# Activation stores two tiles ahead, and another order of loads, eviction and casts at the change of halves

## The reference, cut to what matters

```python
h = rmsnorm(x, g_pre) * (1 + scale[:, None]) + shift[:, None]
z = h @ w_in
a_conv, g_conv, q, k, v, g_attn, qi, ki, wi, gm = split_in(z)
y_c, conv_new = conv_branch(a_conv, conv_prev, conv_w, conv_b, ln_g, ln_b)
y_c = (y_c * jax.nn.silu(g_conv)) @ w_conv_out
o = sparse_attention(q, k, v, qi, ki, wi, past, rel_bias)
y_a = (o * jax.nn.silu(g_attn)) @ w_attn_out
gm_c, gm_a = jnp.split(jax.nn.sigmoid(gm), 2, axis=-1)
y = rmsnorm((gm_c * y_c + gm_a * y_a) @ w_out, g_post)
return x + gate[:, None] * y, conv_new, k, v, ki
```

## Time and profile before

| | us |
|---|---|
| median of 3 runs | 3480.4 (3471.67 to 3483.89) |
| the profiled execution | 3479.13 |
| its span in the trace | 3477.5 |
| PE busy | 3268.8 (94%) |
| DVE busy | 2691.2 (77%) |
| ACT busy | 1466.0 (42%) |
| POOL busy | 1037.6 (30%) |

### The profile page before, as it was taken

How to read it: one execution, slowest core, us unless ns; L and a number is a source line. 1 busy time by engine, 2 the same in 40 slices (tenths; PEclk the granted TensorE clock), 3 DMA queues, 4 the chain that set the end, 5 groups by cost and what they waited for, 6 DMA issues and landing times. The chain is left out here.

```text
span 3477.5 us, 50401 instructions
## 1 busy us (share of the span) xinstructions
PE 3268.8 (94%) x19461; PEld 3008.9 (87%) x19461; DVE 2691.2 (77%) x4071; ACT 1466.0 (42%) x1961; POOL 1037.6 (30%) x885
## 2 busy tenths in 40 slices
PE   6999999999999999999998999898999989999998
PEld 3889888999999899999996777777777779989987
DVE  2432788998989899999995888898898875886444
ACT  2312567988930100010004666676676650323121
POOL 2222111453335300000003443543533324664200
PEclk9999999999999999999999999999999999999999
DMA  7265534545555643344444322323221235667443
GB/s 262 76 181 161 150 118 130 165 148 191 174 187 183 250 151 145 141 170 156 166 147 109 91 56 65 80 56 86 57 61 52 58 112 179 202 210 267 136 145 112
DMA packets 381524, 485.53 MB, mean 140 GB/s; under 512 B 49296, under 2 KB 304464, under 8 KB 379685
## 3 DMA queue, kind: packets, MB, share of 16 engines
q1 hardware_dynamic: 324133, 288.19, 27.7%
q10 hardware_dynamic: 46960, 152.90, 12.5%
q0 software_dynamic: 10256, 42.23, 3.0%
HBM read 301.98 MB, written 184.13 MB: 140 GB/s over the span
## 5 line engine op out<-in xcount | busy, mean ns | idle before, releaser
L1126 PE MATMUL psum<-ha,gt 128*128 128x352 f32 x8136 | 1350.9, 324 | 5.1 <-DVE ha L1402 3.6
L1126 PEld LDWEIGHTS psum<-ha,gt 128*128 128x128 f32 x8136 | 1321.1, 188 | 8.7 <-DVE ha L1402 3.8
L1438 DVE SCALAR_TENSOR_TENSOR cv<-cv,vecs,cv 128x1056 f32<-128x1056 f32 (+1 forms) x480 | 607.7, 1346 | 0.0
L1912 ACT CAST at<-psum 128x1024 fp32r<-128x1024 f32 (+2 forms) x308 | 288.9, 938 | 318.8 <-PE psum L1823 318.5
L1986 DVE TENSOR_TENSOR at<-psum,at 128x1024 fp32r<-128x1024 f32 (+2 forms) x308 | 345.9, 1127 | 80.2 <-ACT at L1912 78.3
L1823 PE MATMUL psum<-ident,at 128*128 128x128 f32 (+1 forms) x2320 | 346.5, 276 | 39.8 <-ACT at L1893 30.3
L1842 PE MATMUL psum<-at,at 128*128 128x512 f32 (+1 forms) x1160 | 343.2, 399 | 27.3 <-ACT at L1920 26.8
L1823 PEld LDWEIGHTS psum<-ident,at 128*128 128x128 f32 (+1 forms) x2320 | 275.8, 143 | 102.3 <-ACT at L1893 37.7
L703 PE MATMUL psum<-br,br 128*128 128x352 f32 x2016 | 340.6, 330 | 14.9 <-DVE br L2359 10.7
L703 PEld LDWEIGHTS psum<-br,br 128*128 128x128 f32 x2016 | 334.0, 192 | 18.6 <-issue 12.0
L777 DVE TENSOR_SCALAR_CACHE_REDUCE gl<-gt,gl 128x1792 bf16<-128x1792 f32 (+8 forms) x263 | 337.7, 1350 | 1.2
(11 more groups left out here) (253 smaller groups left out, 4143.3 us busy)
## 6 DMA issues: line engine op xcount, KB each, us to landing
scratch_ws<-gt SPq DMA_DIRECT2D x112, 512.0 KB, 4.0
gt<-scratch_ws ACTq DMA_DIRECT2D x110, 512.0 KB, 5.0
gt<-in_w_in_dram SPq DMA_DIRECT2D x60, 512.0 KB, 5.8
scratch_gm<-gt ACTq DMA_DIRECT2D x32, 528.0 KB, 3.0
br<-scratch_gm ACTq DMA_DIRECT2D x32, 528.0 KB, 3.8
scratch_m<-br POOLq DMA_DIRECT2D x32, 528.0 KB, 5.1
at<-scratch_q SPq DMA_DIRECT2D x128, 128.0 KB, 2.9
scratch_u<-gl POOLq DMA_DIRECT2D x16, 528.0 KB, 4.2
```

The costliest lines, as they stand in the source:

```text
L1126: return nc.tensor.matmul(of[:, j, 0:W // 3], part[:, c, :], a[:, c, j * (W // 3):(j + 1) * (W // 3)], start=(c == 0 and k == 0), stop=(c ...
L1438: ins = nc.vector.scalar_tensor_tensor(to[:, 0:width], mine[:, k_:k_ + width], tap, to[:, 0:width], ALU.mult, ALU.add)
L1912: nc.scalar.copy(phi[j % 3][:, 0:len(mine), 0:n], turned[j % 2][:, 0:len(mine), 0:n]).then_inc(s_phi, 1)
```

## The change

In the front stage SP's step `t` issues `hidden(t + 2)` instead of `hidden(t + 1)`; since tiles below 8 are not stored, the first store moves from step 7 to step 6.

In the gate stage ACT issues `fetch(BLOCKS + 1)` ahead of the eviction of block `BLOCKS - 2` instead of behind it and behind `fetch(BLOCKS)`. This fetch now waits for the store of the block that it reads, no longer for the last store of split weights. In `next_acts` all casts stand behind the eighth load, so that the eviction of the last block stands ahead of every cast.

```diff
--- before.py
+++ after.py
@@ -321,8 +321,8 @@
                 if t >= 1:
                     key_columns(t - 1)
                 key_rows(t)
-                if t + 1 < NTL:
-                    hidden(t + 1)
+                if t + 2 < NTL:
+                    hidden(t + 2)
                 if 0 <= t - FREE < len(LOADS):
                     query_weights(t - FREE)
             key_columns(NT)
@@ -1266,10 +1266,10 @@
                         act.wait_ge(pr.s_split, QI - E + BLOCKS)
                     else:
                         act.wait_ge(pr.s_mm, QI - E + (j - 2 if j == BLOCKS + 2 else j - 1))
-                    if j <= BLOCKS + 2:
+                    if j == BLOCKS or j == BLOCKS + 2:
                         act.wait_ge(s_wst[0 if j == BLOCKS else 1], 16 * BLOCKS)
                     if j == BLOCKS + 1:
-                        act.wait_ge(s_wst[0], 32)
+                        act.wait_ge(s_wst[1], 32)
                     done = s_wfirst[j - BLOCKS - 1] if BLOCKS < j <= BLOCKS + 2 else s_wld[j % 2]
                     for k, part in enumerate(later(j)):
                         act.dma_start(part[:].rearrange("p c f -> p (c f)").bitcast(F32), scr["ws"][j - BLOCKS, k]).then_inc(done, 16)
@@ -1283,10 +1283,7 @@
                         act.wait_ge(pr.s_mm, QI - E + BLOCKS)
                         evict(BLOCKS // 2 - 1, 1)
                     act.dma_start(alo[:, c, :].bitcast(F32), scr["h"][:, c, W:2 * W]).then_inc(s_act[c], 16)
-                    if c >= 3 and c < KC - 1:
-                        next_high(c - 3)
-
-                for c in range(KC - 4, KC):
+                for c in range(KC):
                     next_high(c)
 
             def next_high(c):
@@ -1337,10 +1334,11 @@
                 if j == BLOCKS - 1:
                     next_acts()
                 else:
+                    if j == BLOCKS - 2:
+                        fetch(BLOCKS + 1)
                     evict(j // 2, j % 2)
                 if j == BLOCKS - 2:
                     fetch(BLOCKS)
-                    fetch(BLOCKS + 1)
                 elif j == BLOCKS - 1:
                     fetch(BLOCKS + 2)
                 elif j > BLOCKS:
```

## The result

| | median us | ratio to the kernel before, 95% interval |
|---|---|---|
| first comparison, 4 runs each | 3453.2, before 3479.5 | 0.9930 (0.9912 to 0.9948) |
| again, 7 runs against 12, on another occasion | 3459.7, before 3478.6 | 0.9952 (0.9936 to 0.9969) |

The change is a gain of 0.5 to 0.7%: 26 us by the first comparison (interval 18 to 31), 19 by the second (11 to 22). The forecast was 3460, a gain of 19.0. The profiled execution of the first comparison took 3456.8 us, span 3455.1; that of before 3479.1. The two traces therefore differ by 22.4 us of span.

The account below looks back on a forecast made before the run. In the front, late-issued stores of h held DVE's modulate and so PE; at the change of halves PE waited for ACT's eviction behind casts. Savings 15.3 + 3.7 = 19.0 us from 3479.1 gave 3460 us; range 3450 to 3471.

Parts of the forecast that it names:

- The waits for `h` go: Front stage: issuing the store of h a tile sooner removes all 22.4 us of DVE's modulate waits.
- What is late next in the front: Tiles 9 to 16: PE's steps of 52.8 us plus two delays make 55.3 instead of 70.6; 15.3 us saved.
- root chain: Front: scale factors of tiles 12 to 15, made on DVE behind modulate(11), delay PE by 1.8 us.
- second weight block: Front: ACT's cast of the second early weight block waits for its load, tile 14's cast queues behind; 0.7 us.
- Edit 2: Change of halves: spare weights fetched first; nothing on PE's path by itself, later activation rows some 1.3 us sooner.
- Edit 3: Change of halves: eviction before casts; one PE gap of 4.4 us replaces 3.56 and 5.13, pair ends 5.1 us sooner.
- The dump: After the pair: weights ACT fetches beside POOL's mask dump come late, cutting the 5.1 us gain to 3.7.
- The other reading: At the dump: if DMA queues' turns were equal in bytes, weights come in time and the gain is 5.1 us.
- (a): Rival: only the front counts, dump or landings take the whole gain at the change of halves; 3464; chance 0.12.
- (c): Rival: key outputs' round on SP, about 9.5 us a tile, bounds the front, not the stores; 3471; chance 0.08.
- (b): Rival: short gaps remain in the front and the clock falls in two; front 10.4, in all 14; 3465; chance 0.12.
- (d): Rival: ACT's seventh load stalls at issue, delaying eviction, clock low for the pair; 10.5 us slower, 3490; chance 0.03.

Follow-up runs that it names:

- e5: Kernel before with one swap in SP's front-stage step: the store of h (still tile t + 1) ahead of the key rows; one run, 3462.8 us.
- e8: Changed kernel plus two front edits: root chain ahead of modulate on DVE, second early weight block cast one step later on ACT; 3452.1 us, ratio 0.9917.
- e3: Kernel before with only the casts moved behind the eviction, spare weights' fetch left where it was; 3471.5 us, ratio 0.9990.
- e4: Kernel before with only the spare weights' fetch ahead of the eviction and its loosened wait, casts as before; 3473.7 us, ratio 0.9988.
- e14: Changed kernel with the mask dump in four stores, one behind each of blocks 3 to 6 of half two; one run, 3457.7 us.
- e15: e3 with the mask dump in four stores, one behind each of blocks 3 to 6 of half two; one run, 3461.9 us.
- e2: Kernel before with both gate-stage edits (spare weights first, eviction ahead of casts), without the front's edit; 3472.4 us, ratio 0.9988.
- e12: The changed kernel repeated unaltered against the kernel before on the same chip; 3459.7 us, ratio 0.9952.
- e9: e3 with the mask dump cut into eight stores of 4.6 KB a row instead of one of 37 KB a row; one run, 3477.2 us.

## Why the prediction was right, step by step

- **The waits for `h` go.** Right: 22.4 us to none, and e5 shows that the loop of modulation, copies, issues and landing was the bound and the key outputs were not.
- **What is late next in the front.** 15.3 was forecast as 70.6 - 55.3; the stretch is 55.7 to 56.1 in the four kernels with this edit and the old delays, 14.6 to 14.9 less than before. The term for the root chain, 1.8, measured 1.82 in all four. That for the second weight block, 0.7, measured 0.95 to 1.32; it was the term that was too small, and it follows the landing: from issue to cast that load took 5.15 us before and 5.57 to 5.95 in the four. e8 takes both delays away and comes to 52.9, where 52.8 was reckoned. One reading of the time before was wrong: the slow product, 9.14 us instead of 6.7, was no cost on top of the loop, as e3 and e4 show. The forecast of 15.3 does not use it.
- **Edit 2.** This step was wrong in its size. I said that nothing of it is on PE's path by itself and that the later landings come 1.3 us sooner. They came 2.8 us sooner at the fifth cast (8.1 us after the last block, the load had landed after 10.9 before), and alone the edit is worth 3.3 us at the fourth block (e4). The step that failed is the reckoning by idle DMA, 1.4 us of transfer pulled forward: I left out that PE's first gap and the dump both hang on the landings.
- **Edit 3.** The gap was reckoned at 4.4 and is 4.44; the pair at 29.3 after the last block and is 29.0 to 30.2. The price of the clock after the gap was taken at 1.5; it was 2.5 in the trace after and 1.3 to 1.6 in the others with both edits. Alone it is worth nothing by the mark (e3), for just the reason that the prediction gave as late next.
- **The dump.** The mechanism, that the weights fetched beside the dump come late, was right and is borne out by e14 and e15; its terms were not. The dump was issued 22.2 to 23.0 us after the last block where 24.6 was reckoned, since the activations landed sooner and POOL's parts took 13.0 instead of 13.9 us. It took 13.0 us in the trace after, but 13.7 in e2 and 15.1 in e12 and e8. So it landed 35.2 to 38.1 us after the last block, where 37.6 was reckoned. The weights landed 6.8, 6.2, 5.2 and 5.3 us behind it, where I took 5.3. That 5.3 does not follow from the prediction's own words: with 10% of the rate for ACT, 2.7 us more beside the dump are worth 0.3 us and not the 1.4 that it took off 6.7, and the gain would have been 2.7 instead of 3.7. It was in part luck, then, that the fourth block was forecast at 43.0 and came at 42.3 and 43.6. The wait of 1 to 3 us that was to be seen there came in e2, e8 and e12; in the trace after it was 0.4, as the pair had ended a microsecond later. In full, 3.4 to 4.7 us saved against 3.7 forecast. The other reading, that turns equal in bytes would bring the weights in time and leave 5.1, is answered by e9: with packets of 4 KB they were still late.
- **The rivals.** (a) is out by the marks of e2, (c) by e5. (b): the clock stayed at 1.00 with gaps of up to 1.6 us, and in e5 with one of 2.4. (d): ACT's eight loads did not hold up the eviction, which came at once. Their chances, 0.35 together, went to things that the trace had nearly excluded.
- **The sum.** 19.0 forecast; 19.2 by the marks of the first pair of traces, 18.9 by the second comparison, 26.3 by the first. The first median lies 7 us under the forecast, inside the range of 3450 to 3471 but near its end; no part of the kernel that the change touches holds those 7 us, and the untouched stretches alone spread by more. That the second comparison met the forecast to 0.1 us is luck, as its interval is 11 us wide.

## What to carry to other kernels

Count the length of the loop that goes through a buffer's store: modulation, the queue's earlier issues, the landing. It costs nothing below the bound engine's own step, and everything above it; slow stretches of that engine cost nothing on top while the loop holds it. Two cheap moves broke it here equally well: storing one step ahead, or issuing the store before its neighbours in the queue. And when a stall is taken away, look which transfer the next wait hangs on before booking the gain: here the eviction's 5 us were worth nothing until a background dump came sooner or was spread out.

## What the runs showed of the hardware

- A wide background store holds up loads beside it for its whole length: 4.7 MB took 12.8 to 15.2 us, and 0.5 MB loads of weights that have a median of 5.0 us in this kernel took 6.3 to 13.5 beside it, the longer the earlier they were issued (5.4 and 6.7 in e14, with the dump later). Even ACT's issue of such a load then took up to 3.7 us (0.4 and 0.9 in e14). Cutting the store's rows from 37 KB to 4.6 KB brought the weights 0.5 us sooner; four pieces, issued a block of 11.65 us apart, took away all of PE's wait.
- Executions differ by some 10 us up to the first product, and by 12 us in a stage of 940 us, without any difference in code there. A change of 5 us is seen in the marks of a trace, which repeat to 0.4 to 1.9 us, and hardly in twelve timed runs.
- Behind gaps of PE of about 4.4 us the first piece of nine matmuls took 2.5 to 3.0 us instead of 1.6, and the second 1.6 to 2.8; 1.3 to 2.5 us were lost. Gaps of up to 1.6 us left nothing slow. Behind gaps of 2.1 to 3.3 us a product of 6.7 us took up to 9.4, but not always: behind 2.37 (e4), 2.39 (e5) and 2.1 us (tile 16's product in before, e2, e9 and e15) it took 6.7.
